# A hybrid encoder layer on one core: merge weights and mixer tiles loaded during the last attention, merged columns taken early, output projection over six PSUM banks

## The reference

```
h      = rmsnorm(x) * (1 + scale) + shift                  # scale, shift, gate from c
q, k, v, rx, rg, ga, gb = split(h @ w_in)
attn   = chunk-band attention(q, k, v, relative bias)      # 8 heads of 64, 512 columns
rnn    = rg_lru(conv4(rx)) * gelu(rg)                      # 512 columns
merged = sigmoid(ga) * (attn @ w_branch[:512]) + sigmoid(gb) * (rnn @ w_branch[512:])
x      = x + gate * (merged @ w_out)
h      = rmsnorm(x) * (1 + scale2) + shift2
up     = conv3(h @ ffn_up_w);  x = x + gate2 * ((val * gelu(gt)) @ ffn_down_w)
y      = rmsnorm(x) * g
```

## Time and profile before

| what | value |
|---|---|
| median of 3 runs | 3026.63 us (3025.68 to 3028.2) |
| the profiled execution | 3025.76 us, of which its span 3024.0 us |
| PE busy | 2851.1 us (94% of the span) |
| DVE, ACT, POOL busy | 1545.7, 1076.0, 49.3 us |
| mean granted TensorE clock | 0.974 |
| DMA | 226.68 MB, mean 75 GB/s |

### The profile page before, as it was taken

One profiled execution on the slowest core, in us unless ns is written; L12 is line 12 of the kernel. 1 busy time (PEld: TensorE's weight loads), 2 busy tenths in 40 slices (PEclk: granted clock), 3 DMA queues, 4 the chain that ended last, 5 costly groups with the idle time before them and its releaser, 6 DMA issues.

```text
span 3024.0 us, 52727 instructions
## 1 busy us (share of the span) xinstructions
PE 2851.1 (94%) x20144; PEld 1820.2 (60%) x20144; DVE 1545.7 (51%) x2761; ACT 1076.0 (36%) x1973; POOL 49.3 (2%) x37
## 2 busy tenths in 40 slices
PE   5799998998996999999799899999999999999998
PEld 3367467476574444444599566666666666666665
DVE  3756355463653343333477676666666666211112
ACT  4345335444443111111255554444444444100000
POOL 0000000000000000000011200000000000000000
PEclk9899999999998999999899899999999999999999
DMA  7110111001004222221445111111111116533211
GB/s 278 38 36 2 53 37 35 32 23 46 35 9 192 70 70 75 79 84 49 138 122 144 56 57 56 56 56 56 56 56 56 56 58 229 149 92 91 89 42 39
DMA packets 168519, 226.68 MB, mean 75 GB/s; under 512 B 49408, under 2 KB 126720, under 8 KB 165840
## 3 DMA queue, kind: packets, MB, share of 16 engines
q1 hardware_dynamic: 158336, 213.50, 21.4%
q10 hardware_dynamic: 8992, 8.76, 0.8%
q0 software_dynamic: 1072, 2.65, 0.2%
HBM read 164.00 MB, written 63.50 MB: 75 GB/s over the span
## 4 chain that ended last, share of the span: by engine, by line
PE 83%; DVE 7%; ACT 4%; issue 4%; DMA 1%; DVEq 0%; SPq 0%; ACTq 0%
PE ps L2082 44%; PE ps L2055 17%; PE ps L1896 11%; PE ps L1933 3%; PE ps L1973 3%; PE ps L1960 2%; DVE arena L1613 1%; ACT arena L941 1%; PE ps L1947 1%; PE ps L1913 1%; PE ps L1858 1%; DMA arena<-mixer_outputs 1%; ACT arena L827 1%; DVE arena L1280 1%; PE ps L1848 1%
## 5 line engine op out<-in xcount | busy, mean ns | idle before, releaser
L2082 PE MATMUL ps<-arena 128*128 128x352 f16 (+1 forms) x11016 | 1489.8, 298 | 31.1 <-DMA arena<-merged 16.4
L2082 PEld LDWEIGHTS ps<-arena 128*128 128x128 f16 x11016 | 1026.5, 97 | 493.6 <-issue 19.1
L2055 PE MATMUL ps<-arena 128*128 128x512 f16 (+1 forms) x2880 | 519.7, 343 | 20.6 <-DVE arena L1501 12.9
L2055 PEld LDWEIGHTS ps<-arena 128*128 128x128 f16 x2880 | 241.7, 97 | 298.6 <-issue 19.5
L1896 PE MATMUL ps<-arena 128*128 128x512 f16 (+1 forms) x1920 | 355.4, 348 | 30.5 <-DVE arena L1280 19.1
L1896 PEld LDWEIGHTS ps<-arena 128*128 128x128 f16 x1920 | 163.5, 99 | 222.5 <-issue 37.7
L1793 DVE SCALAR_TENSOR_TENSOR arena<-ps,arena 128x352 f32<-128x352 f32 (+1 forms) x64 | 30.0, 491 | 352.3 <-PE ps L2082 303.0
L1512 DVE SCALAR_TENSOR_TENSOR arena<-ps,arena 128x512 f32<-128x512 f32 (+1 forms) x80 | 47.6, 599 | 301.6 <-PE ps L2055 299.1
L1001 ACT ACTIVATE arena<-ps 128x352 f32<-128x352 f32 x264 | 119.5, 463 | 199.5 <-PE ps L2082 199.5
L820 ACT ACTIVATE arena<-arena 128x640 f32<-128x640 f32 (+5 forms) x136 | 103.8, 763 | 211.7 <-DVE arena L1429 211.7
L1177 ACT ACTIVATE arena<-arena 128x352 f32<-128x352 f32 x48 | 23.9, 498 | 408.7 <-DVE arena L1793 408.7
(11 more groups left out here) (186 smaller groups left out, 2422.3 us busy)
## 6 DMA issues: line engine op xcount, KB each, us to landing
arena<-in_w_up SPq DMA_DIRECT2D x44, 512.0 KB, 4.1
ffn_hidden<-arena SPq DMA_DIRECT2D x44, 512.0 KB, 3.2
arena<-in_w_in SPq DMA_DIRECT2D x38, 512.0 KB, 5.2
arena<-ffn_hidden SPq DMA_DIRECT2D x5, 3872.0 KB, 19.8
arena<-in_w_mod_rest SPq DMA_DIRECT2D x32, 512.0 KB, 3.2
arena<-in_w_down SPq DMA_DIRECT2D x7, 1408.0 KB, 6.2
arena<-mixer_outputs SPq DMA_DIRECT2D x8, 1056.0 KB, 15.5
arena<-in_x_cols SPq DMA_DIRECT2D x12, 704.0 KB, 4.6
```

The source lines that it names most:

```text
L2055: mm = pe.matmul(out, wt[:, wp, k, :], act_t[:, k, hp, t:t + w], start=(k == k0 and m == 0), stop=(k == k1 - 1 and m == 2))
L2082: mm = pe.matmul(out, wt[:, k, wp, :], act_t[:, k, hp], start=(first and k == 0 and n == 0), stop=(last and k == K - 1 and n == 2), skip_g ...
```

## The change

On the host the tiles of `w_in` are put in another order, so that the two weight tiles which the last round of the head-pair loop loads and splits are gate tiles 0 of the merge; the SBUF map is moved so that `wst`/`wsp` are the first slots of `dst`/`dsp`, and so that the buffers of the attention lie above the first six tiles of `mixT`.

SP now loads the first branch weight and the mixer tiles 0, 1, 2, 4, 5 and 6 before it waits for the end of the last attention, tile 7 after it, and tile 3 after its store, which ACT issues. PE's first gate products wait for no split after attention, the branch products come in the order 1, 0 and wait for seven tiles, then for the last. The 32 modulation tiles are taken in eight blocks running, not in twice four. Most of the output weights have buffers of their own and are brought and split earlier; the last merged tile is copied on ACT from `mstage`; PE takes e = 0 whole, tile m by tile m, and the blocks after it go over banks 0, 1, 2, 3, 6, 7.

```diff
-WQ, WK, WV, WRX, WRG, WGA, WGB = 0, 4, 8, 12, 16, 20, 28
+WRX, WGA, WQ, WGB, WRG, WK, WV = 0, 4, 12, 16, 24, 28, 32
...
+        MIX = {0: 0, 1: 1, 2: 2, 4: 3, 5: 4, 6: 5, 7: 6, 3: 7}
...
+        def e_bank(u):
+            return u if u < 8 else (0, 1, 2, 3, 6, 7)[(u - 8) % 6]
...
@@ SP, end of the head-pair loop, and after it
-                sp.wait_ge(ot_ready, (NT + 1) * (j + 2))
-                sp.dma_start(mix_d[ds(j, 1)].rearrange("j p s t -> (j p) s t"), ost).then_inc(attn_stored, 16)
+            sp.wait_ge(kf_stored, 32 * (NJ + 1))
+            sp.wait_ge(rnn_stored, 32 * (NJ + 1))
+            sp.wait_ge(attn_stored, 16 * NJ)
+            sp.dma_start(dst[:, 2], a["w_branch"][0]).then_inc(d_loaded[2], 16)
+            for k in (0, 1, 2, 4, 5, 6):
+                mixer_tile(k, mix_loaded)
             sp.wait_ge(ot_ready, (NT + 1) * (NJ + 1))
             sp.wait_ge(v_stored, 32 * (NJ + 1))
+            mixer_tile(7, mix_loaded)
-            merge_tiles(0, 0)
             sp.wait_ge(attn_stored, 16 * (NJ + 1))
+            mixer_tile(3, mix_last)
+            merge_tiles(0, 1)
...
@@ SP, end of the merge
+            for n in range(28, 31):
+                later_tile(n)
+            sp.wait_ge(d_split, 3 + 3 * KT)
+            out_tile(0)
+            sp.wait_ge(d_filled, 40 + 20 * (KT - 1))
+            out_tile(1)
+            out_tile(2)
+            sp.wait_ge(m_stored, 64 * KT)
+            merged_tile(mT01[0], 0, 0, KT - 1, mt_a0)
+            later_tile(31)
+            sp.wait_ge(e_split, 1)
+            out_tile(3)
+            sp.wait_ge(e_split, 4)
+            out_tile(4)
             sp.wait_ge(d_filled, 40 + 20 * KT - 2)
+            out_tile(5)
+            merged_tile(mT01[1], 1, 0, KT - 1, mt_b0)
+            out_tile(6)
+            sp.wait_ge(e_split, 5)
+            out_tile(7)
             sp.wait_ge(d_filled, 40 + 20 * KT)
             sp.wait_ge(m_stored, 64 * KT + 64)
...
@@ ACT
+                act.wait_ge(ot_ready, (NT + 1) * (j + 2))
+                act.dma_start(mix_d[ds(j, 1)].rearrange("j p s t -> (j p) s t"), ost).then_inc(attn_stored, 16)
...
+            def last_tile_part(e, t):
+                act.wait_ge(d_mlo, 5 * (KT - 1) + t // 512 + 1)
+                act.activation(mT01[e][:, KT - 1], mstage[:, :, t:t + CE], ACT.Copy).then_inc(mt_last, 1)
...
+                        if last and q == 1 and n == 1:
+                            last_tile_part(0, 0)
                         if last and q == 1 and n >= 2:
-                            out_hi_part(n - 2)
+                            for k in ((0, 1, 2), (3,), ())[n - 2]:
+                                out_hi_part(k)
...
-            merge_hi(0, 0)
+            act.sem_inc(d_hi, 2)
+            act.wait_ge(d_loaded[2], 16)
+            act.activation(dsp[:, 2, 0], dst[:, 2], ACT.Copy, scale=WS).then_inc(d_hi, 1)
...
@@ DVE
-                        if n < 4:
-                            adaln_tile(it, 4 * q + n)
+                        if 5 * q + n < 8:
+                            adaln_tile(it, 5 * q + n)
+                        if 5 * q + n == 7:
+                            dve.wait_ge(dm_step, 16 * it + 17)
+                            dve.tensor_copy(modraw[:, ds(16 * it, 16)], dsum).then_inc(dm_kept, 1)
+                            if last:
+                                gate_columns()
+                        if last and q == 1 and n >= 2:
+                            for k in ((0, 1, 2), (3,), ())[n - 2]:
+                                out_lo_part(k)
...
@@ PE, merge
-                    pe.wait_ge(d_split, 6 * it + 3 * q + 6)
+                    pe.wait_ge(d_split, 6 * it + 3 * q + 5)
...
-                        pe.wait_ge(mix_loaded, 16 * KT)
-                        for m in range(2):
+                        if n == 0:
+                            pe.wait_ge(d_split, 6 * it + 3 * q + 6)
+                        for m in (1, 0):
+                            pe.wait_ge(mix_loaded, 16 * (KT - 1)) if m else pe.wait_ge(mix_last, 16)
...
@@ PE, output projection
-            pe.wait_ge(d_dve, 4 + 10 * KT)
-            pe.wait_ge(d_act, 4 + 10 * KT)
...
             for m in range(KT):
+                if m in (0, 4):
+                    pe.wait_ge(d_act, 4 + 10 * KT - (0 if m else 2))
+                    pe.wait_ge(d_dve, 4 + 10 * KT - (0 if m else 2))
                 pe.wait_ge(e_split, m + 1)
-                passes(ps[:, m, 0:CE], wo[m], mT01[:, 0], 0, KT - 1, KT, True, False, None)
-            pe.wait_ge(mt_a0_last, 16)
-            for m in range(KT):
-                passes(ps[:, m, 0:CE], wo[m], mT01[:, 0], KT - 1, KT, KT, False, True, e_filled)
+                passes(ps[:, m, 0:CE], wo[m], mT01[0], 0, KT, KT, True, True, e_filled)
...
-                    pe.wait_ge(e_x1, 8 * e + m - 3)
+                    pe.wait_ge(e_x1, 8 * e + m - 5)
```

More of the change, by code:

```diff
@@ L319, in build @@
         mt_a0 = sem("mt_a0")
-        mt_a0_last = sem("mt_a0_last")
+        mt_last = sem("mt_last")
+        mix_last = sem("mix_last")
         mt_b0 = sem("mt_b0")
@@ L713, in _ @@
                         act.wait_ge(ss_ready, i - 1)
-                    act.activation(junk[0:rows, i % 2], x_all[0:rows, i, :], ACT.Square,
+                    act.activation(junk[0:rows, i % 2], x_of(i)[0:rows, :], ACT.Square,
                                    accum_out=rstd[0:rows, i:i + 1]).then_inc(ss_ready, 1)
@@ L720, in _ @@
                     act.wait_ge(xT_filled, i + 1)
[L721 removed]
+                    act.activation(xT_of(i)[:, 4:8, 0:rows],
                                    ps[:, 2 * (i % 2) + 1, :].rearrange("p (k t) -> p k t", t=P)[:, :, 0:rows],
@@ L740, in _ @@
                     rows = P if i < NT else TS
-                    act.activation(hT[:, :, 0, i * P:i * P + rows], xT[:, i, :, 0:rows], ACT.Copy)\
+                    act.activation(hT[:, :, 0, i * P:i * P + rows], xT_of(i)[:, :, 0:rows], ACT.Copy)\
                         .then_inc(hi_ready, 1)
@@ L871, in merge_hi @@
                 for i in range(3):
-                    act.wait_ge(d_loaded[i], 16 * f + 16)
+                    act.wait_ge(d_loaded[i], 16 * f + 16 if i == 2 else 16 * f)
                     if i == 0:
@@ L917, in _ @@
             merge_body(KT // 2 - 1, True)
-            for k in range(3, KT):
+            act.wait_ge(d_filled, 40 + 20 * KT)
+            last_tile_part(1, 1024)
+            for k in range(4, KT):
                 out_hi_part(k)
@@ L1270, in modulate_block @@
                 for k in range(KT):
-                    ins = dve.tensor_scalar(xT[:, tiles, k, 0:rows], xT[:, tiles, k, 0:rows],
+                    x = xT_all[:, tiles, k, :] if n < 4 else xT_of(NT)[:, k, 0:TS]
+                    ins = dve.tensor_scalar(x, x,
                                             coefv[:, 0, 0, src, k:k + 1], coefv[:, 0, 1, src, k:k + 1],
@@ L1560, in _ @@
             merge_body(KT // 2 - 1, True)
-            dve.wait_ge(dm_kept, 1 + KT // 2)
-            chain(rows_of(modraw[:, 16:64], 1, 0, 24))
-            coefficients(1)
-            for m in range(2):
-                for s in range(2):
-                    ins = dve.tensor_scalar(gcolv[:, m, s], modv[:, m, 16:24, s], CS, None, ALU.mult)
-            chain(ins)
-            for k in range(3, KT):
+            for k in range(4, KT):
                 out_lo_part(k)
@@ L1580, in x_new @@
                     if src == 0 or e >= 2 * NE - 2:
-                        bank = m if e == 0 else m % 4
+                        bank = e_bank(8 * e + m)
                         ins = dve.scalar_tensor_tensor(xb[h][:, m, t0:t1], ps[:, bank, t0:t1], gcolv[:, 0, src, m:m + 1],
@@ L2231, in lay_out @@
         "w_mod_rest": np.concatenate([i["mod_mix_w"][0][:, 2 * D:3 * D].T, i["mod_ffn_w"][0].T]).reshape(32, P, D),
-        "w_in": tiles(i["w_in"][0]),
+        "w_in": tiles(i["w_in"][0])[[*range(12, 16), *range(20, 28), *range(0, 4), *range(28, 36), *range(16, 20),
+                                      *range(4, 12)]],
         "cache_k": np.ascontiguousarray(i["cache_k"].reshape(4, P, NJ, P)),
```

131 lines of the change are left out of this document (65 added, 66 removed).

## The result

| | before | after |
|---|---|---|
| median of 4 runs | 3027.16 us (3025.68 to 3028.2) | 2994.39 us (2993.03 to 2994.86) |
| the profiled execution, its span | 3025.76, 3024.0 us | 2993.03, 2991.2 us |
| mean granted clock | 0.974 | 0.980 |

The ratio of the times is 0.9891, 95% interval 0.9879 to 0.9902: 32.8 us less, where 36.1 were forecast. 2990.5 was the prediction, with a range of 2983 to 3001; the time lies within it.

The account below looks back on a forecast made before the run. PE, busy 94% of the span, was taken as the bound, with three waits of 36.9 us to remove. Gains of 21.9 and 14.2 us made 36.1 off 3026.6, so 2990.5 us, range 2983 to 3001.

Parts of the forecast that it names:

- First hand-over: Attention to merge: PE starts at 936.6 at half clock, first block ends at 954.5; gain 21.9 us, bounds 14.3 to 24.4.
- so short a pause would have left it up: Rival at the merge's start: clock stays up through a 1.5 us pause, 2.5 us less, 2988; chance 0.15.
- The cover of tile 3: Merge's first block: the last mixer tile lands at 947.5, wanted at 952.0, so 4.5 us to spare.
- The rival that named the longer store: Attention to merge: store shares with tile 7's load, last mixer tile late, 7.6 us more, 2998; chance 0.10.
- The rows of c: Merge start: they delay first evacuations to about 956, PE needs those banks at 970; no cost.
- the modulation tiles in eight blocks: Merge: each tile costs DVE 2.5 us and a 3.2 us transfer, DVE half idle; charged nothing.
- The slower case: Rival in the merge: PE stops each round for modulation tiles through one buffer, 3040 us; chance 0.02.
- Second hand-over: Merge to output projection: PE goes on without pause, then waits 2.2 and 1.7 us for weights; gain 14.2, bounds 7.6 to 18.2.
- lands 5.0 later: Output projection's start: weight 4, issued at 1477.8, lands 5.0 us later, at 1482.8, the median landing.
- The sign that I had set: Whole kernel: clock at 0.50 for about 5 us at the merge's start and nowhere else until the feed-forward.
- the third rival: Output projection's start: output weights come late, 6.6 us more, 2997; chance 0.15.
- The banks: Output blocks after the first: PE waits for no bank, so six banks gain nothing; 1.23 us pauses at `sum_squares` remain.

Follow-up runs that it names:

- `banks4`: The changed kernel with four PE banks again instead of six in the blocks after the first; 2995.22 us, ratio to before 0.9895.
- `w4_early`: The changed kernel with output weights 4 to 7 issued together earlier, weight 4 in its own buffer and split before ACT's stores, x rows issued earlier; 2988.91 us.
- `t7_after_store`: The changed kernel with mixer tile 7 issued only once the store of the attention's rows has landed; 2995.03 us, one run.
- `late_gates`: The changed kernel, but PE waits for all eight mixer tiles before its first gate products; 3006.32 us, one run.
- `t3_late`: The changed kernel with mixer tile 3 issued behind three weight tiles and the rows of c; 3001.68 us, one run.
- `both_banks4`: The kernel `both` with four banks instead of six; 2987.69 us, ratio to before 0.9869.
- `w6_first`: The changed kernel with output weight 6 issued ahead of the merged tiles of block 1, not behind them; 2994.4 us, ratio to before 0.9894.
- `both`: `w4_early` plus DVE, not ACT, opening the merge's first blocks, and block 1's merged tiles issued after block 0's x rows; 2987.15 us, again 2986.71.

## Why the prediction was right, and where its terms were off

*First hand-over, forecast 21.9, measured 21.4.* Right by its steps. PE's start was put at 936.6 and was at 936.50; no pause in the first 72 matmuls; the clock was down, as the row of before had said. By the rule in the Trainium skill ("TensorE: Matmul & The Clock Gate", Part 1) as I had read it, so short a pause would have left it up; here the measurement decides. It stayed down 5.8 us and not 5.0, so 2.9 were lost and not 2.5; that this came so near is luck, since the same stretch was between 2.7 us (`banks4`) and 6.0 us (`w4_early`, `t7_after_store`) long in the other runs. `late_gates` shows what the early start is worth: without it 11.9 come back. The cover of tile 3 was put at 4.5 us and was 3.9. Two errors stand against each other in it: the store took 8.0 us beside tile 7 where I had carried over 5.66 from a trace with other traffic, and the load behind it took 4.8 where I had 6. The rival that named the longer store was right about the mechanism and wrong in that it would matter. `t3_late` shows what happens past the limit. The rows of c were late too: the first evacuation began at 960.59 where I had 956, and PE wanted those banks only at 970. The six early loads were charged nothing, and that holds: from the store of the last values (849.51 before, 849.25 after) to the last split of the attention it is 85.9 us in both.

*The merge.* Nothing for the modulation tiles in eight blocks was right: their landing is 3.2 us after as before, and the merge without its pauses and slow stretches is as long as before: 1475.43 - 947.99 less a pause of 7.6 and twice 2.5 of clock is 514.8 us, 1454.05 - 936.50 less 2.9 of clock is 514.7. The slower case needed landings of 33 us.

*Second hand-over, forecast 14.2, measured 10.4.* Here a term was mis-sized: "lands 5.0 later", the median over all eight output weights, for the weights on the path, which took 3.3 (weight 4), 11.7 (weight 6) and 8.0 us (weight 7). The pauses were forecast as 2.2 us before m = 4 and 1.7 before m = 7; they were 1.24 before m = 4 and 5.19 before m = 6, plus 1.5 us of clock lost around the latter, where I had charged no clock and given no reason for it. The sign that I had set, no 0.50 anywhere else before the feed-forward, failed with it; for pauses about as short as the two that I forecast the clock did stay up (1.24 us here, 1.81 in `both_banks4`). Weight 4 was a little better than forecast. Weight 6 I had not looked at: it went behind the merged tiles of block 1 and beside the stores of the last column, and landed after 11.66 us. In sum 7.9 us against 3.9, 4.0 more; 0.2 of it is a pause in the second output block (at 1508.74 before) that is gone, which leaves the 3.8 that are missing. This is the third rival in part (it had 7.6 as that part's gain): the mechanism, weights queued behind stores and merged tiles, at a little over half its price and on weight 6 where it named 4 and 7. `w6_first` shows that the place in the line mattered to weight 6 and that weight 7 was nearly as late behind it; `w4_early` and `both`, that asking for all of them earlier takes these waits away.

*The banks, forecast nothing.* `banks4` and `both_banks4` bear this out within 1 us. The pauses at `sum_squares` stand unchanged after, 0.89, 1.23, 1.22, 1.23 and 1.59 us.

*The sum.* 0.5 less at the first hand-over, 3.8 less at the second and 0.9 more in the feed-forward, which I had at nothing, make the 36.1 forecast 32.7; the profiled executions differ by 3025.76 - 2993.03 = 32.7. The 0.9 can't be assigned to an edit: it is the remainder of clock and pauses in the feed-forward, and the last section says how far two executions of one kernel differ in such places.

## What to carry to other kernels

Take the landing of a transfer from its own place in the queues, not from the median of its kind: list what is issued on any queue in the ten microseconds before it, and add the bytes. In `w6_first` a reordering of transfers only brought out the wait for the next weight; a buffer of its own, so that the request could go out earlier, removed both. When a long wait is taken away, walk the same chain again with the new start times until the first item that has no cover; here that was weight 6, then the x rows, then the merged tiles, which held PE for 5.2, 2.5 and 0.7 to 1.8 us.

## What the runs showed that I had not expected

**Two large transfers on two queues.** The 1 MB store took 4.0 us alone and 8.0 beside a load of 1 MB, about 0.27 MB per us in sum either way.

**The clock after a short pause.** After the attention it fell with pauses of 1.65 us and of 1.02 us. In the output projection, where PE had been busy without a gap, it stayed at 1.00 through 1.24 us (kernel after), 1.54 (`w6_first`), 1.68 (`banks4`) and 1.81 (`both_banks4`), and fell with 2.51 (`w4_early`). In the feed-forward it fell with 2.71 us in the kernel before and stayed up with 2.71 in the kernel after. So the length of the pause alone does not decide it; that the thinly filled tail of the attention is the difference is my reading, and no run fills that tail to test it. The time that the clock stayed low differed with no edit in between: the changed kernel run again gave these stretches.

```profile
937.00:938.00 1.00, 0.33 (x1) 0.14 (x1) 0.25 (x2) 0.23 (x1) 0.00 (x0) 1.00 0.00 0
938.00:939.00 1.00, 0.00 (x0) 0.00 (x0) 0.21 (x1) 0.00 (x0) 0.00 (x0) 0.89 0.00 0
939.00:940.00 1.00, 0.66 (x2) 0.28 (x3) 0.00 (x0) 0.50 (x1) 0.00 (x0) 0.50 1.56 127
...
942.00:943.00 1.00, 1.00 (x6) 0.42 (x5) 0.00 (x0) 0.00 (x0) 0.00 (x0) 0.91 1.01 422
```

PE restarted at 939.34 and the clock was up by about 942.2, 2.8 us later, where the first profile had 5.8 us from a start at 936.50. The attention also ended 2.8 us later in that profile. All of this had come about before anything that the change moves: the recurrence's store of the third head pair was already 2.9 us later (623.67 against 620.77), and 1.4 of it lies in one run of 240 matmuls behind the first turn of the loop, 45.96 us against 44.59. One execution differs from another by a few microseconds in this way, and single runs should not be read closer than that. Why the clock is up sooner in one execution than in another is open.

**Short rows.** 616 KB of merged tiles took 9.9 us where 512 KB of weights takes 3 to 6: the former are read in rows of 176 elements, 352 bytes. Whether it is the rows or the traffic around them no run separates.
